# LayerNorm's weight and offset folded into the adaLN modulation of a two-layer mLSTM and MoE decoder, with x rebuilt on GpSimd

## What is computed

```python
cond = silu(c)
for l in range(2):
    sh1, sc1, gt1, sh2, sc2, gt2 = split(cond @ w_ada[l] + b_ada[l], 6)
    u = x * (1 + sc1) + sh1
    proj = u @ w_in[l]                       # q, k, v, o, gates, conv: 3592 columns
    h = mlstm_chunkwise(q, k, v, i, f)       # 4 heads of 128
    h = head_norm(h, mh_norm_w[l]) * sigmoid(o)
    y_conv = b_gate * causal_conv3(c_gate * h_in)
    mix = concat(h, y_conv) @ w_out[l]
    x = layer_norm(ALPHA * x + (1 + gt1) * mix, ln1_g[l], ln1_b[l])
    u = x * (1 + sc2) + sh2
    y = hier_moe(u)                          # best of 4 groups, best 2 of its 4 experts
    x = layer_norm(ALPHA * x + (1 + gt2) * y, ln2_g[l], ln2_b[l])
```

## Time and profile before

| | |
|---|---|
| median of 3 runs | 863.11 us (862.99 to 864.66) |
| profiled execution | 866.84 us, of which its span is 865.1 us |
| mean granted TensorE clock | 0.973 of full speed |
| busy share of TensorE, VectorE, ACT, GpSimd | 95%, 40%, 12%, 3% |
| moved by DMA | 299.29 MB, mean 346 GB/s |
| in the page's slices of the expert loops | 410 to 416 GB/s, TensorE 90% or more |

### The profile page before, as it was taken

The page is one execution under the profiler, slowest core; times in us unless marked ns, Lnnn a source line. Parts: engine busy times, 40 slices in busy tenths (PEclk is TensorE's granted clock), DMA queues, the critical chain, the costliest instruction groups (busy, mean ns, idle before and its releaser), DMA issues.

```text
span 865.1 us, 9037 instructions
## 1 busy us (share of the span) xinstructions
PE 822.0 (95%) x3774; PEld 438.1 (51%) x3782; DVE 348.2 (40%) x739; ACT 99.7 (12%) x234; POOL 28.7 (3%) x72
## 2 busy tenths in 40 slices
PE   7799999998999999999979999989899999999994
PEld 3485488475444344434337748845444434443431
DVE  0188878865111111121153995685521111111115
ACT  2111000013101010101021100001311001010110
POOL 2070000000000000000000000000000000000000
PEclk9999999988999999999989999999999999999997
DMA  8999998567999999999999599425799999999991
GB/s 298 389 341 381 387 387 298 216 248 291 354 397 416 410 413 415 412 411 415 414 388 334 207 359 386 183 98 187 280 388 397 415 412 412 415 415 409 414 396 52
DMA packets 90653, 299.29 MB, mean 346 GB/s; under 512 B 4153, under 2 KB 4441, under 8 KB 82417
## 3 DMA queue, kind: packets, MB, share of 16 engines
q1 hardware_dynamic: 86960, 291.60, 86.7%
q0 software_dynamic: 2592, 7.04, 2.2%
q10 hardware_dynamic: 1056, 0.03, 0.1%
HBM read 297.60 MB, written 1.05 MB: 345 GB/s over the span
## 4 chain that ended last, share of the span: by engine, by line
PE 81%; DMA 10%; DVE 3%; issue 2%; SPq 2%; ACT 0%; DVEq 0%
PE bank L588 23%; PE bank L546 13%; PE bank L612 12%; PE bank L575 7%; PE bank L765 6%; PE bank L632 6%; DMA ring<-in_w_in_dram 5%; PE bank L563 5%; DMA ring<-in_w_up_dram 3%; DMA ring<-in_w_ada_dram 2%; SPq L355 2%; PE bank L481 2%; PE bank L524 1%; PE bank L596 1%; PE bank L460 1%
## 5 line engine op out<-in xcount | busy, mean ns | idle before, releaser
L546 PE MATMUL bank<-uT,ring 128*128 128x256 f32 x640 | 142.2, 383 | 2.1 <-DMA ring<-in_w_in_dram 2.1
L546 PEld LDWEIGHTS bank<-uT,ring 128*128 128x128 f32 x640 | 122.1, 192 | 22.5 <-issue 3.1
L588 PE MATMUL bank<-ring,qT 128*64 128x512 f32 x512 | 113.1, 594 | 2.8 <-issue 2.8
L612 PE MATMUL bank<-ring,hb 128*64 128x512 f32 x512 | 113.4, 595 | 1.4 <-ACT hb L878 1.4
L588 PE MATMUL bank<-ring,uT 128*64 128x512 f32 x512 | 112.9, 594 | 0.3 <-DMA ring<-in_w_up_dram 0.3
L997 DVE SCALAR_TENSOR_TENSOR acc<-ring,cond,acc 128x512 f32<-128x512 f32 x112 | 84.2, 752 | 4.0
L612 PEld LDWEIGHTS bank<-ring,hb 128*64 128x64 f32 x512 | 35.3, 137 | 76.3 <-issue 74.6
L588 PEld LDWEIGHTS bank<-ring,qT 128*64 128x64 f32 x512 | 36.8, 137 | 70.9 <-issue 69.9
L588 PEld LDWEIGHTS bank<-ring,uT 128*64 128x64 f32 x512 | 36.1, 137 | 71.2 <-issue 68.5
L575 PEld LDWEIGHTS bank<-ccT,X 128*128 128x128 f32 x512 | 61.5, 197 | 13.2 <-issue 11.4
L575 PE MATMUL bank<-ccT,X 128*128 128x128 f32 x512 | 64.6, 285 | 0.2
(11 more groups left out here) (234 smaller groups left out, 561.9 us busy)
## 6 DMA issues: line engine op xcount, KB each, us to landing
ring<-in_w_gate_dram SPq DMA_DIRECT2D x32, 2048.0 KB, 17.2
ring<-in_w_up_dram SPq DMA_DIRECT2D x32, 2048.0 KB, 16.4
ring<-in_w_down_dram SPq DMA_DIRECT2D x32, 2048.0 KB, 16.3
ring<-in_w_ada_dram SPq DMA_DIRECT2D x24, 2048.0 KB, 19.8
ring<-in_w_in_dram SPq DMA_DIRECT2D x14, 2048.0 KB, 18.4
ring<-in_w_out_dram SPq DMA_DIRECT2D x4, 2048.0 KB, 15.2
gate_row<-in_b_ada_dram POOLq DMA_DIRECT2D x4, 512.0 KB, 8.6
ln_g<-in_ln_g_dram POOLq DMA_DIRECT2D x4, 512.0 KB, 10.9
```

What stands on the lines that cost most here:

```text
L546: last = pe.matmul(bank[4 + (b0 + q) % 4][:, 0:SEQ], w[:, kc, q * P:(q + 1) * P], uT[:, kc, :], start=(kc == 0), stop=(kc == KC - 1))
L588: last = pe.matmul(bank[bk][CAP * j:CAP * (j + 1), :], xg[b][:, 4 * h + k, CAP * j:CAP * (j + 1)], ring[s[h]][:, 4 * j + k, :], start=(h = ...
L612: last = pe.matmul(bank[6 + half][CAP * j:CAP * (j + 1), :], hhT[:, f, CAP * j:CAP * (j + 1)], ring[s[h]][:, 4 * j + 2 * i + half, :], sta ...
```

## The change

LayerNorm's result is x = n * g + b, with n = (x - mean) * rstd. The next modulation u = x * (1 + sc) + sh is written as u = n * (g * (1 + sc)) + (b * (1 + sc) + sh). So:

- `finish` writes only n, in one pass with two scalars; `centre` is gone. The same in `last_norm` of layer 0, where VectorE writes the left half of the channels and ACT the right half. `last_norm` of layer 1 stays.
- `shift_scale` makes the folded scale and shift from g and b as columns (`norm=`); `mod` gets two more rows, because the gathered columns of the MoE still need the plain ones. g and b as columns come by six more small loads and transposes (`small_columns`).
- GpSimd's `rebuild` turns n into x in place, two passes per half (times `ln_g`, plus `ln_b`), once the half has been transposed. The gather, ACT's filling of PSUM with alpha x and layer 1's `add` wait for it (`x_full`).
- The one-column matmuls of `moe_columns` and `early_columns` become `four_sums` (four matmuls of 32 output partitions and 512 columns side by side), an ACT copy, and `four_columns` (four transposes). Layer 1's sums move from between the transposes to behind the routing logits, and VectorE's part behind the first `build_disp`.
- VectorE and ACT share the modulation of both halves of the MoE's uT, four chunks each.
- SP issues the first two adaLN units ahead of the small loads; the small transposes stand behind adaLN unit 1.
- GpSimd's row and routing loads of layer 0 wait for projection unit 4 instead of 1; those for LayerNorm 2 wait for `x_full`.
- The counts of zero matmuls change: 3 and 6 around each adaLN unit (before 5), 18 ahead of layer 1's transposes (before 0), 7 between the MoE's transposes (before 5 and 13); the four zero matmuls that clear PSUM are spread.

```diff
+            def rebuild(l, which, t):
+                pool.wait_ge(xT_ready, 8 * l + 4 * which + 2 * t + 2)
+                pool.tensor_tensor(X[:, t, :], X[:, t, :], ln_g[:, :], ALU.mult).then_inc(x_scaled, 1)
+                pool.wait_ge(x_scaled, rebuilt(l, which) + t + 1)
+                pool.tensor_tensor(X[:, t, :], X[:, t, :], ln_b[:, :], ALU.add).then_inc(x_full, 1)
...
                 if l:
-                    pool.wait_ge(x_ready, 2 * T * l)
-                arrived(pool, "proj", l, 1)
+                    pool.wait_ge(rows_landed, 16 * 5 * l)
+                    for t in range(T):
+                        rebuild(l, 0, t)
+                    pool.wait_ge(x_full, rebuilt(l, 1))
+                arrived(pool, "proj", l, 4 if l == 0 else 1)
                 load_rows(l, 0)
...
-                pool.wait_ge(x_ready, 2 * T * l + T)
+                pool.wait_ge(rows_landed, 16 * (5 * l + 3))
+                for t in range(T):
+                    rebuild(l, 1, t)
+                pool.wait_ge(x_full, rebuilt(l, 1) + T)
                 load_rows(l, 1)
...
+            def four_sums(bk, l, units, done):
+                for g, i in enumerate(units):
+                    last = pe.matmul(bank[bk][32 * g:32 * g + 32, :], ones[:, 0:32], weighed_sums(l, i),
+                                     start=True, stop=True, tile_position=(0, 32 * g))
+                last.then_inc(done, 1)
+            def four_columns(bk, sums, pieces, done):
+                for q, cols in enumerate(pieces):
+                    last = pe.transpose(bank[bk][:, q * P:(q + 1) * P], sums[:, cols], ident[:, :])
+                last.then_inc(done, 1)
...
             def ada_units():
                 for i in range(4):
                     ada_unit(i)
-                    if i:
-                        pe.wait_ge(ada_part, i)
-                        columns(6, i - 1, partials, part[:, (i - 1) % 2, :], in_ext)
+                    if i == 1:
+                        small_columns()
+                    stay_busy(3, 3)
+                    pe.wait_ge(ada_part, i + 1)
+                    columns(6, i, partials, part[:, i % 2, :], in_ext)
                     if i < 3:
-                        stay_busy(5, 3)
...
+                        stay_busy(6, 3)
...
-                moe_columns(l)
+                pe.wait_ge(weighed, turn(l, 9))
+                four_sums(6, l, (4, 5, 8, 9), moe_sum)
                 transpose_half(0, x_ready, 2 * T * l + 1, rows_of)
-                if l == 0:
-                    early_columns()
-                stay_busy(5 if l == 0 else 13, 5)
+                pe.wait_ge(moe_copied, l + 1)
+                four_columns(6, moe_sums, even_odd, moe_ext)
+                stay_busy(7, 5)
                 transpose_half(1, x_ready, 2 * T * l + 2, rows_of)
...
+                if l == 0:
+                    pe.wait_ge(early_weighed, 4)
+                    four_sums(7, 1, range(4), early_sum)
                 gate_row_half(l, GATE2)
                 if l == 0:
-                    pe.wait_ge(mod_in_ready, 2)
-                stay_busy(5)
+                    pe.wait_ge(early_copied, 1)
+                    four_columns(7, early_sums, in_turn, early_ext)
+                else:
+                    stay_busy(5)
...
+                pe.wait_ge(x_full, rebuilt(l, 1) + T)
                 gather(main, PAIRS * l, 0)
...
+                if l + 1 < DEPTH:                                   # last_norm, VectorE
+                    for t in range(T):
+                        newton(t, 1, rs_ready, T * (2 * l + 1) + t + 1)
+                        dve.scalar_tensor_tensor(out=nmr[:, t:t + 1], in0=mv[:, t, 0:1], scalar=-1.0, in1=rstd[:, t:t + 1],
+                                                 op0=ALU.mult, op1=ALU.mult).then_inc(nmr_ready, 1)
+                        dve.tensor_scalar(X[:, t, 0:COLS], bank[2 * t][:, :], mv[:, t, 0:1], rstd[:, t:t + 1],
+                                          ALU.subtract, ALU.mult).then_inc(x_ready, 1)
+                    return
...
+                if norm:                                            # shift_scale
+                    link(last)
+                    weight, offset = norm
+                    link(dve.tensor_tensor(fold_shift[:, :], mod[:, 2 * which + 1, :], offset, ALU.mult))
+                    dve.tensor_tensor(mod[:, 4 * which, :], mod[:, 2 * which, :], fold_shift[:, :], ALU.add)
+                    last = dve.tensor_tensor(mod[:, 4 * which + 1, :], mod[:, 2 * which + 1, :], weight, ALU.mult)
...
                 def finish(t):
                     newton(t, 1, rs_ready, 2 * T * l + t + 1)
-                    dve.scalar_tensor_tensor(out=X[:, t, :], in0=X[:, t, :], scalar=rstd[:, t:t + 1],
-                                             in1=ln_b[:, :], op0=ALU.mult, op1=ALU.add).then_inc(x_ready, 1)
-
+                    dve.tensor_scalar(X[:, t, :], X[:, t, :], mv[:, t, 0:1], rstd[:, t:t + 1], ALU.subtract, ALU.mult).then_inc(x_ready, 1)
```

More of the change, by code:

```diff
@@ L281, in weighed_sums @@
             return acc[:, (i - 4) if i < GATE2 else (i - 8), :]
+        moe_sums = expo[:, :, :].rearrange("p h s -> p (h s)")[:, 2 * COLS:3 * COLS]
+        early_sums = part[:, 0, :]
+        even_odd = [slice(h * SEQ + j, (h + 1) * SEQ, 2) for h in range(2) for j in range(2)]
+        in_turn = [slice(q * P, (q + 1) * P) for q in range(4)]
         def turn(l, i):
@@ L342, in _ @@
             sp.dma_start(c_rows, c.rearrange("a (k p) -> (a k) p", p=P)).then_inc(c_landed, 16)
+            for n in range(2):
+                sp.dma_start(ring[n][:, :, :], unit_source(("ada", 0, n))).then_inc(landed[n], 16)
             for l in range(DEPTH):
@@ L487, in gate_row_half, with small_columns @@
                 pe.matmul(bank[4 + i % 2][:, :], ones[:, :], weighed_sums(l, i), start=True, stop=True).then_inc(row_ext, 1)
[L489 to L499, removed]
+            def four_sums(bk, l, units, done):
[7 more added lines that the diff above has]
+                last.then_inc(done, 1)
+            def small_columns():
+                pe.wait_ge(cols_landed, 16 * (5 * DEPTH + 2))
+                for i in range(DEPTH):
+                    pe.transpose(bank[7][:, 64 * i:64 * i + NMOD], b_ada_rows[:, i, :], ident[0:NMOD, 0:NMOD])
+                    for k in range(4):
+                        pe.transpose(bank[7][:, 192 + 32 * i + 8 * k:200 + 32 * i + 8 * k],
+                                     b_moe_rows[:, i, k // 2 * SEQ + k % 2:(k // 2 + 1) * SEQ:2], ident[0:8, 0:8])
+                    last = pe.transpose(bank[7][:, 128 + 16 * i:128 + 16 * i + 3 * CH], w_conv_rows[:, i, :],
+                                        ident[0:3 * CH, 0:3 * CH])
+                last = pe.transpose(bank[7][:, 256:256 + 2 * KC], ln2_rows, ident[0:2 * KC, 0:2 * KC])
+                last.then_inc(cols_ready, 1)
             def ada_units():
@@ L957, in _ @@
                     ln_rsqrt(l, 1, t)
+                if l + 1 < DEPTH:
+                    for t in range(T):
+                        act.wait_ge(nmr_ready, T * l + t + 1)
+                        act.activation(X[:, t, COLS:2 * COLS], bank[2 * t + 1][:, :], ACT.Identity,
+                                       bias=nmr[:, t:t + 1], scale=rstd[:, t:t + 1]).then_inc(hat_act, 1)
         @block.vector
@@ L1167, in _ @@
                         last = dve.tensor_copy(w_conv_col[:, i, :], bank[7][:, 128 + 16 * i:128 + 16 * i + 3 * CH])
+                    last = dve.tensor_copy(ln2_col[:, :, :], bank[7][:, 256:256 + 2 * KC].rearrange("p (v k) -> p v k", v=2))
                     last.then_inc(cols_copied, 1)
                     dve.wait_ge(cols_copied, 1)
+                    for which in range(2):
+                        at = 3 * KC * which + KC
+                        last = dve.tensor_scalar(b_ada_col[:, :, at:at + KC], b_ada_col[:, :, at:at + KC], 1.0, None, ALU.add)
+                    last.then_inc(cols_copied, 1)
+                    dve.wait_ge(cols_copied, 2)
                 if l == 0:
                     dve.wait_ge(in_ext, 4)
-                    shift_scale(0, 0, 6, mod_in_ready)
+                    first_shift_scale()
                 dve.wait_ge(mod_in_ready, l + 1)
```

124 lines of the change are left out of this document (74 added, 50 removed).

## The result

The changed kernel takes 854.89 us (median of 6 runs, 852.92 to 858.53); the kernel before, on the same chip, 863.29. The ratio is 0.9906, with an interval of 0.9882 to 0.993: faster by 0.94%, or 8.4 us. The forecast was 21.4 us and a range that ends at 851, so the sign was right and the time lies outside the range. The profiled execution took 855.74 us (span 854.0, mean granted clock 0.987) against 866.84: 11.1 us less. The profiled execution of before lay 3.55 over the median of before, that of the changed kernel 0.85 over its own, so the profiles differ by more than the medians do.

A forecast was written before the change was run, and what follows sets the result against it. TensorE, busy 95%, was taken as the bound, the weight stream second. Gains 6.6 + 10.0 + 4.3 + 3.8, less 1.5 and 1.8, made 21.4 us: 866.84 to 845.4 profiled, 841.7 from the median; range 836 to 851.

The forecast's parts named there:

- I charge 0.9 a layer: Output projection to gather, both layers: GpSimd's passes and VectorE share memory, costing 0.9 us a layer, 1.8 in all.
- R1: Rival: GpSimd passes hold VectorE off between output projection and gather, gather at M + 17.3; sum 17.3, 845.8 us; chance 0.28.
- M: End of a layer's output projection; before the change, the gather started 23.78 us later in layer 0, 17.42 in layer 1.
- stretch A: Start to layer 0's last conv block: 6.6 us gained, 3.8 before the projections and 2.8 from GpSimd's moved loads.
- R2: Rival: stretch A gains only 2.3 to 3, the stream or a clock fall limiting it; sum 17.5, 845.6 us; chance 0.14.
- The 3.8 of the start: Start to first projection: 3.8 us earlier through earlier adaLN loads, zero matmuls and moved columns; bounds 2.26 and 3.8.
- C: Seam from layer 0's LayerNorm 2 to layer 1's projections: 4.3 us gained, bounds 3.4 and 4.8.
- the stream, -1.5: Layer 0's expert loop: the earlier gather leaves weight stream owed, a loss of 1.5 us, bounds 0 and 2.7.
- B and D: Output projection to gather in layers 0 and 1: gather at M + 13.6, gains of 10.0 and 3.8 us.
- R3: Rival: the norm's pass is not shorter and the clock still falls before the gather; sum 15.9, 847.2 us; chance 0.06.
- R4: Rival: the gather waits for slow GpSimd passes; at 6 us a pass the time is 867; chance 0.03.

The follow-up runs named there:

- no_pass: Changed kernel with GpSimd's passes that rebuild x left out, so the gather works on normalized n; 846.40 us (one run).
- late_pass: Changed kernel with GpSimd's LayerNorm 1 passes also waiting until VectorE has finished both halves of x; 856.95 us (one run).
- one_input: Changed kernel with the modulation fold and Newton's steps rewritten to take no second input from SBUF; 848.82 us (one run).
- early_pass: Changed kernel with each half's first GpSimd pass not waiting for the transposes and writing to another buffer; 849.53 us (one run).
- split_early_one: Changed kernel with the edits of early_one and split_rows together, nothing left out; 839.32 us (5 runs), ratio to before 0.9735.
- experiments 1 to 9: The first nine of eleven follow-up kernels, each an edit or combination of edits on the changed kernel; 839.32 to 856.95 us.
- rows1: Changed kernel with GpSimd's row and routing loads waiting for projection unit 1 again, as before; 855.98 us (4 runs), ratio to before 0.9907.
- early_one: Changed kernel with the edits of one_input and early_pass together; 848.79 us (4 runs), ratio 0.9817.
- split_rows: Changed kernel with layer 0's ln_g, ln_b and routing loads moved behind a later adaLN unit; 851.57 us (4 runs), ratio 0.9866.

## Why the prediction was wrong, step by step

**The step that failed: "I charge 0.9 a layer, about half a pass in the way of one small VectorE instruction: 1.8."** The passes cost 5.5 us a layer (19.0 and 18.84 less no_pass's 13.47 and 13.32), 11.0 in both. The failed term is a cost put far too low because the wait behind it was not believed: the rival R1 is what happened. I had priced it rightly in kind and gave it 0.28, because no row of before showed a held instruction; but no row of before could, since GpSimd has no tensor work beside VectorE there (its selects end at 8.13, and VectorE's first instruction with an input starts at 8.76). That is an absence of evidence that I weighed as evidence against. The Trainium skill (SBUF — State Buffer, Who interferes with whom) says that a VectorE instruction with two SBUF inputs contends with a GpSimd one that reads SBUF, not with one that only writes it. By that rule the trace and four experiments agree: held to 1.56 to 2.37 us with two SBUF inputs (the changed kernel, late_pass, one_input's routing, early_pass), 0.17 with one from PSUM or beside a GpSimd that only writes.

R1's own price was short by 1.7 a layer (M + 17.3 against 19.0). A pass takes 2.35 us, not 1.9, and x of half 1 was ready at M + 8.5 where R1 had M + 7.8: 0.7. TensorE's clock, which R1 left at full, adds 0.76 for the transposes and 0.43 for each of two sets of routing matmuls (1.06 against 0.63 in split_early_one): 1.6. The held block in the routing that R1 had at 1.0 was hardly there (`ahead` 0.44 in place of 0.33; from the logits to the gather 4.12, in split_early_one 3.85): 0.7 less. That is 1.6 of the 1.7.

**The 2.8 of stretch A.** Only 0.43 came. The wait of 2.09 that I read in the earlier trace rows went away (a smaller one, 1.04, stands at 118.61), but I did not ask what the loads would meet at their new place: "The loads that move are wanted some 25 us after they now start" is true of them and says nothing of what they delay. They stood ahead of the next adaLN unit, and VectorE, then TensorE at the end of the mixer, waited for it. Placed behind that unit they give 4.0 more (143.71 to 139.68), so some 4.4 against before, where 2.8 was forecast. The bounds of 0 to 3.2 were too narrow as well. R2 (A not delivered) had the size nearly right, 2.3 to 3 where 1.84 came, but not this cause.

**The 3.8 of the start.** It came as 1.41 here. Over ten profiled kernels with this code at the start (the changed one and experiments 1 to 9) the first projection lies between 36.29 and 38.43, mean 37.44: a gain of 2.4. The earliest, 36.29 in one_input with all four units at 1.92, is a gain of 3.5. I had taken for the value what was the upper bound. The earlier load is there (issued at 1.27, as forecast), but the first unit is not taken up when it lands: TensorE is still at ten zero matmuls, which took 3.99 us in the changed kernel and 2.33 in one_input. Whether one more unit then runs at half clock decides the rest (the third took 2.51 in the changed kernel, and the six zero matmuls ahead of it 2.50 in place of 1.46). "SP's issue takes 0.3 to 0.4 us each" was wrong for the first of the small loads behind the two units: it took 3.82 (2.35 to 6.17); nothing in the changed kernel waited for it.

**The seam, C, and the stream, -1.5.** Together forecast at 2.8, measured 3.35, and now they can be taken apart. From the start of the last expert sums on TensorE to the first projection it is 16.5 us before (441.12 to 457.6) and 13.2 after (434.43 to 447.6): C is 3.3, not 4.3: from the last variance to x ready on VectorE 3.7 are gained (446.01 to 452.7 before, 439.32 to 442.3 after), and from x to the projections 0.4 are lost, where I had expected a gain. From the gather to those sums it is 233.3 before (207.82 to 441.12) and 233.2 after: nothing was owed to the stream. Even with the gather at 189.85, the loop and seam of split_early_one take 246.4. The charge of 1.5 was 0, its lower bound. The seam's clock is as forecast; the window of the changed kernel:

```profile
443.00:448.00 5.00, 3.88 (x37) 2.37 (x35) 2.91 (x9) 2.90 (x8) 4.21 (x2) 1.00 1.05 385
```

**B and D without the passes.** M + 13.6 was forecast for both layers; no_pass has 13.47 and 13.32, split_early_one, with the passes, 13.62 twice. The one-tensor pass took 0.81, inside its bounds of 0.69 and 1.28. R3 (pass no shorter) is out; the clock did fall between M and the gather, but behind the wait that the hold makes, and it stays at 1.00 without it. R4 is out too: in the changed kernel the last pass ends at 197.6 and the gather starts at 201.20.

**What is not the change's.** 1.69 of the 11.1 lies in layer 1's projections. That stretch takes 139.7 or 141.4 in these profiles (141.4 in before, no_pass, rows1 and early_one, 139.7 in the changed kernel and the other six of experiments 1 to 9), one block of matmuls at half clock or not. A single profiled run decides nothing of that size; the medians give 8.4. Of the same kind is the clock at the end of layer 0's mixer: with a wait of 3.3 to 3.6 there, it stayed up in the changed kernel and fell in early_one and late_pass, where the stretch takes 147.7. The 0.86 at the end I have not traced.

## What to carry to other kernels

Work that goes to an "idle" GpSimd is paid for by VectorE if both read SBUF: list the VectorE instructions with two SBUF tensor inputs that fall into each pass, and count up to a whole pass for each on the critical path, however small it is (1.56 to 2.37 us here, of passes of 2.2 to 2.5). One input from PSUM, a per-partition scalar in place of a tensor, or a pass placed where VectorE has no such instruction, takes the hold away; here two such edits gave back all but 0.15 to 0.3 us a layer (13.62 against no_pass's 13.47 and 13.32). When loads are moved away from a wait, read the order of the queue at the new place as closely as at the old one: the next unit behind them inherits the wait.

## What the runs showed that I had not expected

- A GpSimd pass over 128x1024 with two inputs takes 2.35 us, 2.19 in the form that reads `zT` and `ln_b` and writes x. The Trainium skill (GPSIMD Engine Reference, Performance versus the Vector engine) had led to an estimate of 2.25 per pass, nearer than my 1.9 from the selects of the earlier trace rows, which have one input.
- A held instruction is booked as busy, from its issue to 0.02 us past the end of the pass for 128x8, and to 0.17 or 0.18 past it for 128x160.
- VectorE's pass over X with one tensor input and two scalars is little disturbed: 1.02 us in one_input, where GpSimd's passes lie beside nearly all of it, 0.85 in split_early_one, where they share 0.3 us, 0.81 alone. In one_input it is GpSimd's pass beside it that grows, to 2.71 us.
- The stream falls while GpSimd's small routing loads land: 289 GB/s in 110 to 120, where this kind of stream runs at 386. The fall goes where they go (321 in 50 to 60 in before, 308 there in rows1, 312 in 130 to 140 in split_rows), while the broadcast rows ahead of them leave it at 392 in 100 to 110.
